# High and low halves of the moving tiles stored apart in a one-core two-block transformer kernel

## The chip, the cores and the metric

The kernel runs on one core of a Trainium2 chip. The metric is the device time of one execution in microseconds. TensorE (PE) multiplies a stationary tile of weights, loaded by its own instruction, with a moving tile that streams from SBUF, and adds into PSUM. VectorE (DVE), ScalarE (ACT) and GpSimd (POOL) work beside it, and SyncE (SP) issues the stream of weights.

## The reference

The reference is two transformer blocks over 256 tokens of width 2048 in float32. Only shapes matter for this change:

```
x:(256,2048)
block 1: h = x + fox_mixer(rms_norm(x))        16 heads of 128, causal softmax with forget decay
         h = h + conv_ffn(rms_norm(h))          up 2048 -> 2*5632, 3-tap conv, silu(gate)*val, down 5632 -> 2048
block 2: x = h + concat(gla, dilated)(rms_norm(h)) @ w_out
         x = x + (silu(h2 @ w_gate) * (h2 @ w_up)) @ w_down
```

Nearly all the arithmetic is in the products with the weight matrices.

## The kernel before

**Products.** Activations are kept transposed: 128 features on the partitions, 256 tokens (`S`) along the row. A product is needed more exactly than one pass of the fp32r format gives, so every weight tile `w` and every activation tile `x` is split into a high part and a low part, and three products are added: `w_hi*x_hi`, `w_hi*x_lo` and `w_lo*x_hi`. Line 391 does the first two in one matmul of 512 columns (256 of the high row, then 256 of the low row) into the two halves of a PSUM bank. Line 394 does the third with 256 columns, the high row alone. Such a pair is called a block here. Blocks go in groups of mostly six: six times line 391, then six times line 394 (`stretch`). The very first half unit does the same on lines 606 and 607, one block at a time.

**Weights.** They come in 784 units of 128 x 1024 through a ring of four buffers: SP loads `raw`, ACT copies it to fp32r `whi` (line 714, `split_hi`), DVE subtracts to get `wlo` (line 1038, `split_lo`), both three units ahead of TensorE. A buffer comes free when TensorE has used it (`unit_used`).

**Moving tiles.** There are three, all with a high and a low row of 256 float32 for each 128-feature chunk: `xs` (16 chunks, the normed input of a projection), `mix` (16 chunks, the heads' outputs, ahead of the output projection) and `hid2` (44 chunks, the hidden layer). ACT writes the high rows (lines 842, 931, 925, 976, 719, 760, 803, 830), DVE the low rows (lines 1061, 1136, 1197, 1269). In the profile's rows `hid2` is called hid, since numbers are left out of names.

**Addresses.** A row of one chunk is 2048 bytes in each partition: the high row, 1024 bytes, then the low row, 1024 bytes. The tile `skipped` puts the start of `xs` at 192 modulo 256 bytes (byte 82112 of each partition), and `arena` gives `hid2` and `mix` the same phase. So every high and every low row starts at 64 modulo 128 bytes, and line 391 reads 2048 bytes without a break. The tiles `whi` and `wlo` start at 128 modulo 256 bytes, and a 128-column slice is 512 bytes, so weights start at a multiple of 128.

**Order.** Each engine's program is written out by hand, in loops; semaphores tie them. There are no pools and no scheduler.

Of the kernel before, what the change touches and what calls it, by code (L numbers as in the profile page):

```python
# [27 lines left out]
F32R = mybir.dt.float32r  # L28
# [6 lines left out]
P = 128  # L35
S = 256
D = 2048
KC = D // P
FF = 5632
FC = FF // P  # L40
# [59 lines left out]
def build(nc, wstream, narrow_w, xt, vectors, identity, dist_onehot, rel_bias, gate_w2, scan_keep, gla_mask, fox_mask, out):  # L100
    with ExitStack() as ctx:
        def sb(name, shape, dt=F32):
            return ctx.enter_context(nc.sbuf_tensor(name, shape, dt))
# [6 lines left out]
        whi = [sb(f"whi{i}", [P, UW], F32R) for i in range(RING)]  # L110
# [1 line left out]
        xres = sb("xres", [P, KC, S])  # L112
        sb("skipped", [P, (X_AT - nc.sbuf_base) % PHASE // 4])
        xs_at = nc.sbuf_base
        xs = sb("xs", [P, KC, 2, S], F32R)
        folded_t = sb("folded_t", [P, S])
        vec = sb("vec", [P, VECTORS])
        ident = sb("ident", [P, P])
# [21 lines left out]
        def place(start):  # L140
            at = [start]

            def put(name, shape, dt=F32):
                t = nc.alloc_sbuf_tensor_at(name, shape, dt, offset=at[0])
                at[0] += int(np.prod(shape[1:])) * 4
                assert at[0] <= nc.sbuf_usable_end, (name, at[0])
                return t
            return put, at

        put, _ = place(arena)  # L150
        hid2 = put("hid2", [P, FC, 2, S], F32R)
        put, at_att = place(arena)
        mix = put("mix", [P, KC, 2, S], F32R)
        at_tables = at_att[0]
        decay_row = put("decay_row", [P, FOX_HEADS, S])
        qk = put("qk", [P, 2, S])
# [15 lines left out]
        put, _ = place(at_gla)  # L172
# [7 lines left out]
        put, at_sq = place(at_tables)  # L180
        sq_all = put("sq_all", [P, KC, S])
        assert at_sq[0] <= at_tables + FOX_HEADS * S * 4
        put, at_tab = place(at_tables)
# [4 lines left out]
        put, _ = place(at_gla)  # L188
# [16 lines left out]
        put, at_z = place(at_tables + FOX_HEADS * S * 4)  # L205
# [11 lines left out]
        def bank(name):  # L217
            return ctx.enter_context(nc.psum_tensor(name, [P, 512], F32))

        acc = [bank(f"acc{i}") for i in range(4)]  # L220
# [150 lines left out]
        def _(pe):  # L371
# [6 lines left out]
            def stretch(pos, blocks, x, *sizes):  # L378

                at = 0  # L380
                assert sum(sizes) == len(blocks)
                for size in sizes:
                    for k, j, bank_no, kc, opens, closes, free, late in blocks[at:at + size]:
                        if j == 0:
                            pe.wait_ge(lo_ready, pos.unit(k) + 1)
                        if free is not None:
                            pe.wait_ge(chunk_out, free)
                        if late:
                            pe.wait_ge(*late)
                        w_hi = whi[pos.slot(k)][:, j * P:(j + 1) * P]  # L390
                        pe.matmul(acc[bank_no][:, :], w_hi, x[:, kc, :, :].rearrange("p a s -> p (a s)"), start=opens, stop=False)  # L391
                    for k, j, bank_no, kc, opens, closes, free, late in blocks[at:at + size]:
                        w_lo = wlo[pos.slot(k)][:, j * P:(j + 1) * P]
                        mm = pe.matmul(acc[bank_no][:, S:2 * S], w_lo, x[:, kc, 0, :], start=False, stop=closes)  # L394
                        if j == BLOCKS - 1:
                            mm.then_inc(unit_used, 1)
                    at += size

            def half(pos, k, bank_no, part, x, late=None):
                stretch(pos, unit_blocks(k, bank_no, part, None, late), x, BLOCKS)  # L400
# [56 lines left out]
            def head(run, pos, h, k0, lag):  # L457

                n = run.count0 + h
                chunk = run.chunk0 + 3 * h  # L460
                stretch(pos, unit_blocks(k0, 1, 0, chunk - 2) + unit_blocks(k0 + 1, 1, 1), xs, 4, 6, 6)
                if lag >= 2:
                    head_values(n - 2, n)
                if lag >= 1:
                    head_scores(n - 1)
                stretch(pos, unit_blocks(k0 + 2, 2, 0, chunk - 1) + unit_blocks(k0 + 3, 2, 1) + unit_blocks(k0 + 4, 3, 0, chunk), xs,
                        4, 6, 6, 6, 2)
                if lag >= 1:
                    head_turn(n - 1)
                stretch(pos, unit_blocks(k0 + 5, 3, 1), xs, 6, 2)  # L470
                if lag >= 2:
                    pe.wait_ge(head_copied, n - 1)
                head_mean(n)
# [125 lines left out]
            def first_half():  # L599
                pe.wait_ge(first_lo, 1)  # L600
                for kc in range(BLOCKS):
                    if kc == BLOCKS // 2:
                        pe.wait_ge(lo_ready, 1)
                    pe.wait_ge(xs_ready, kc + 1)
                    cols = slice(kc * P, (kc + 1) * P)
                    pe.matmul(acc[1][:, :], whi[0][:, cols], xs[:, kc, :, :].rearrange("p a s -> p (a s)"), start=kc == 0, stop=False)
                    mm = pe.matmul(acc[1][:, S:2 * S], wlo[0][:, cols], xs[:, kc, 0, :], start=False, stop=False)
                mm.then_inc(unit_used, 1)

            first = Pos(L0.unit_heads)  # L610
            first_half()
            half(first, 1, 1, 1, xs, {8 + m: (xs_ready, 8 + m + 1) for m in range(BLOCKS)})
            narrow(0)
# [40 lines left out]
            for c in range(6):  # L654
                pe.wait_ge(chunk_out, L1.chunk_in if c == 1 or c == 2 else L1.chunk_heads + c - 2)
                for part in range(2):
                    k = 2 * c + part
# [20 lines left out]
            for j in range(2):  # L678
                chunk = DIL.chunk0 + 3 * j
                n = DIL.count0 + j  # L680
                for c in range(3):
                    pe.wait_ge(chunk_out, chunk + c - 2)
                    for part in range(2):
                        k = 2 * c + part
# [951 lines left out]
```

## Time and profile before

| | |
|---|---|
| median of 3 runs | 2258.39 us |
| the runs | 2257.77, 2258.39, 2271.72 us |
| the profiled execution | 2258.64 us |
| its span, first to last instruction | 2256.9 us |
| PE busy | 2242.0 us, 99% |
| weight loads (PEld) busy | 1968.6 us, 87% |
| DVE busy | 1617.8 us, 72% |
| ACT busy | 1226.5 us, 54% |
| POOL busy | 52.0 us, 2% |
| HBM traffic | 187 GB/s over the span |

The busy time of a matmul in the profile includes the time in which its results drain while the next one already streams, so the durations of matmuls (near 392 ns for 512 columns) overlap. What a matmul costs in a row of matmuls is the distance from its start to the next start.

### The profile page before, as it was taken

How to read it: one execution, taken by the hardware profiler on the slowest of the kernel's cores; microseconds unless marked ns; L12 is line 12 of the kernel's file. 1: busy time of each engine (PE TensorE's matmuls, PEld its weight loads, DVE VectorE, ACT ScalarE, POOL GpSimd, SP SyncE). 2: the span in 40 equal slices, each digit the busy share in tenths (PEclk: the TensorE clock that was granted, in tenths of full speed). 3: DMA queues.
4: the chain of work that ended last, by engine and by line, in shares of the span. 5: the costliest groups of instructions: out<-in, count | busy, mean ns of one | idle time of the engine just before them, and what ended most of it. 6: DMA issues, size and time to landing. Idle time of an engine off the chain costs nothing.

```text
span 2256.9 us, 38996 instructions
## 1 busy us (share of the span) xinstructions
PE 2242.0 (99%) x13138; PEld 1968.6 (87%) x13138; DVE 1617.8 (72%) x2394; ACT 1226.5 (54%) x1614; POOL 52.0 (2%) x78
## 2 busy tenths in 40 slices
PE   7999999999999999999999999999999999999999
PEld 6888888888888888888888888888888888888888
DVE  7877777788888888555567687777666666764554
ACT  6777765655555555444465577655444444443333
POOL 1111100000000000000000000000000000000000
PEclk9999999999999999999999999999999999999999
DMA  5555555555555555555545554455555555556564
GB/s 206 193 174 183 184 176 186 187 195 187 193 196 189 192 186 187 205 192 190 195 162 186 169 174 167 171 186 193 191 192 189 193 195 191 190 191 201 205 198 137
DMA packets 118598, 421.92 MB, mean 187 GB/s; under 512 B 13773, under 2 KB 15973, under 8 KB 118544
## 3 DMA queue, kind: packets, MB, share of 16 engines
q1 hardware_dynamic: 113760, 413.19, 53.8%
q0 software_dynamic: 2048, 5.42, 1.0%
q10 hardware_dynamic: 2736, 2.58, 0.4%
q8 instruction: 35, 0.57, 0.1%
q14 instruction: 19, 0.16, 0.0%
HBM read 419.01 MB, written 3.70 MB: 187 GB/s over the span
## 4 chain that ended last, share of the span: by engine, by line
PE 98%; DVE 1%; ACT 0%; DMA 0%; issue 0%; SPq 0%; DVEq 0%
PE acc L391 63%; PE acc L394 31%; PE b_score L442 0%; PE b_turn L447 0%; DMA xres<-xt 0%; PE b_mean L453 0%; PE b_mean L432 0%; PE b_mean L433 0%; PE b_val L439 0%; PE b_mean L455 0%; PE b_mean L454 0%; PE b_score L441 0%; ACT xs L842 0%; DVE wlo L1038 0%; DVE sq_all L1303 0%
## 5 line engine op out<-in xcount | busy, mean ns | idle before, releaser
L714 ACT ACTIVATE whi<-raw 128x1024 fp32r<-128x1024 f32 x783 | 825.8, 1058 | 821.4 <-PE acc L394 815.4
L1038 DVE TENSOR_TENSOR wlo<-raw,whi 128x1024 fp32r<-128x1024 f32 x783 | 959.5, 1229 | 389.3 <-ACT whi L714 386.6
L391 PE MATMUL acc<-xs,whi 128*128 128x512 f32 x4344 | 1130.7, 394 | 2.2 <-DVE wlo L1038 1.8
L391 PEld LDWEIGHTS acc<-xs,whi 128*128 128x128 f32 x4344 | 765.0, 188 | 124.7 <-DVE wlo L1038 2.9
L394 PEld LDWEIGHTS acc<-xs,wlo 128*128 128x128 f32 x4344 | 608.3, 188 | 64.8
L394 PE MATMUL acc<-xs,wlo 128*128 128x256 f32 x4344 | 620.3, 277 | 0.0
L391 PE MATMUL acc<-hid,whi 128*128 128x512 f32 x1408 | 359.9, 391 | 0.0
L1044 DVE TENSOR_REDUCE folded_t<-acc 128x256 f32<-128x512 f32 x336 | 231.4, 689 | 121.8 <-PE acc L394 110.2
L391 PEld LDWEIGHTS acc<-hid,whi 128*128 128x128 f32 x1408 | 247.2, 188 | 37.9
L394 PEld LDWEIGHTS acc<-hid,wlo 128*128 128x128 f32 x1408 | 194.2, 188 | 19.9
L394 PE MATMUL acc<-hid,wlo 128*128 128x256 f32 x1408 | 197.5, 276 | 0.0
L391 PE MATMUL acc<-mix,whi 128*128 128x512 f32 x512 | 131.5, 393 | 0.0
L391 PEld LDWEIGHTS acc<-mix,whi 128*128 128x128 f32 x512 | 90.4, 188 | 14.9 <-DVE mix L1136 0.5
L394 PEld LDWEIGHTS acc<-mix,wlo 128*128 128x128 f32 x512 | 70.6, 188 | 6.9
L394 PE MATMUL acc<-mix,wlo 128*128 128x256 f32 x512 | 71.9, 277 | 0.0
L830 ACT ACTIVATE hid<-hid 128x256 f32 (+1 forms) x88 | 36.2, 411 | 45.1 <-DVE hid L1265 44.9
L1104 DVE SCALAR_TENSOR_TENSOR qk_n<-qk,qk_gain,rstd_qk 128x256 f32<-128x256 f32 x48 | 21.6, 492 | 44.6 <-ACT rstd_qk L741 44.6
L1078 DVE TENSOR_TENSOR up_g<-folded_t,rstd 128x256 f32<-128x256 f32 x88 | 37.5, 426 | 3.0
L1078 DVE TENSOR_TENSOR up_v<-folded_t,rstd 128x256 f32<-128x256 f32 x88 | 37.5, 426 | 3.0
L1269 DVE TENSOR_TENSOR hid<-hid,hid 128x256 f32 (+1 forms) x88 | 36.9, 419 | 1.0 <-ACT hid L830 1.0
L815 ACT ACTIVATE tap_g<-up_g,vec 128x256 f32<-128x256 f32 x44 | 26.5, 603 | 16.2 <-DVE up_g L1078 16.1
L823 ACT ACTIVATE tap_v<-up_v,vec 128x256 f32<-128x256 f32 x44 | 26.5, 603 | 15.2 <-DVE up_v L1078 15.1
(195 smaller groups left out, 998.8 us busy)
## 6 DMA issues: line engine op xcount, KB each, us to landing
raw<-wstream SPq DMA_DIRECT2D x783, 512.0 KB, 3.3
decay_row<-decay_scratch POOLq DMA_DIRECT2D x16, 128.0 KB, 3.5
out<-xres ACTq DMA_DIRECT2D x16, 128.0 KB, 2.9
xres<-xt SPq DMA_DIRECT2D x3, 512.0 KB, 8.7
dist_scratch<-bias_scratch POOLq DMA_DIRECT2D x8, 192.0 KB, 4.7
toeplitz<-dist_scratch POOLq DMA_DIRECT2D x8, 128.0 KB, 3.3
xres<-xt SPq DMA_DIRECT2D x2, 256.0 KB, 4.6
raw<-wstream SPq DMA_DIRECT2D x2, 256.0 KB, 5.7
```

The costliest lines, as they stand in the source:

```text
L391: pe.matmul(acc[bank_no][:, :], w_hi, x[:, kc, :, :].rearrange("p a s -> p (a s)"), start=opens, stop=False)
L394: mm = pe.matmul(acc[bank_no][:, S:2 * S], w_lo, x[:, kc, 0, :], start=False, stop=closes)
L714: act.activation(whi[slot][:, :], raw[slot][:, :], ACT.Copy).then_inc(hi_ready, 1)
L815: act.activation(tap_g[:, :], up_g[:, 0:S], ACT.Identity, scale=column("conv0", j), bias=column("convb", j)).then_inc(tap0, 1)
L823: act.activation(tap_v[:, :], up_v[:, 0:S], ACT.Identity, scale=column("conv0", FC + j), bias=column("convb", FC + j)).then_inc(tap0, 1)
L830: act.activation(hid2[:, j, 0, :], hid[:, :], ACT.Copy).then_inc(hid_hi_ready, 1)
L1038: dve.tensor_tensor(wlo[slot][:, :], raw[slot][:, :], whi[slot][:, :], ALU.subtract).then_inc(lo_ready, 1)
L1044: dve.tensor_reduce(folded_t[0:rows, :], acc[bank_no][0:rows, :].rearrange("p (a s) -> p s a", a=2), AX_X, ALU.add).then_inc(chunk_folded, 1)
L1078: dve.tensor_tensor(dst, folded_t[0:rows, :], rstd[0:rows, :], ALU.mult).then_inc(chunk_out, 1)
L1104: dve.scalar_tensor_tensor(out=qk_n[:, a, :], in0=qk[:, a, :], scalar=qk_gain[:, col + a:col + a + 1], in1=rstd_qk[:, a, :], op0=ALU.mult, ...
L1269: dve.tensor_tensor(hid2[:, j, 1, :], hid[:, :], hid2[:, j, 0, :], ALU.subtract).then_inc(hid_split, 1)
```

## The change

Each of the three moving tiles is stored as two blocks: first all the high rows, one after another, then a gap of 64 bytes (16 elements), then all the low rows. `xs` and `mix` become 2 x (16 * 256 + 16) elements, `hid2` 2 x (44 * 256 + 16). The indexing `[:, chunk, half, :]` stays as it was, through a rearranged view. The high rows still start at 64 modulo 128 bytes, and the low rows now start at a multiple of 128 bytes. The matmuls of line 391 (and 606) read two runs of 1024 bytes, 16448 bytes apart (45120 in `hid2`), in place of one of 2048; their output is described as two halves of the same PSUM bank, at the same addresses. Line 394 reads the same kind of row as before.

Everything behind `xs` in SBUF moves by 128 bytes; `hid2` and `mix` move by 256 and keep their phase; the tiles behind `mix` move by 384. The weights' buffers and the residual `xres` stay where they are.

```
-        xs = sb("xs", [P, KC, 2, S], F32R)
+        xs = sb("xs", [P, 2, KC * S + 16], F32R)[:, :, 0:KC * S].rearrange("p a (k s) -> p k a s", k=KC)
...
-        hid2 = put("hid2", [P, FC, 2, S], F32R)
+        hid2 = put("hid2", [P, 2, FC * S + 16], F32R)[:, :, 0:FC * S].rearrange("p a (k s) -> p k a s", k=FC)
...
-        mix = put("mix", [P, KC, 2, S], F32R)
+        mix = put("mix", [P, 2, KC * S + 16], F32R)[:, :, 0:KC * S].rearrange("p a (k s) -> p k a s", k=KC)
...
-                        pe.matmul(acc[bank_no][:, :], w_hi, x[:, kc, :, :].rearrange("p a s -> p (a s)"), start=opens, stop=False)
+                        pe.matmul(acc[bank_no][:, :].rearrange("p (a s) -> p a s", a=2), w_hi, x[:, kc, :, :], start=opens, stop=False)
...
-                    pe.matmul(acc[1][:, :], whi[0][:, cols], xs[:, kc, :, :].rearrange("p a s -> p (a s)"), start=kc == 0, stop=False)
+                    pe.matmul(acc[1][:, :].rearrange("p (a s) -> p a s", a=2), whi[0][:, cols], xs[:, kc, :, :], start=kc == 0, stop=False)
```

TensorE's program has the same rows in the same order as before. On DVE and ACT only address arithmetic ahead of writes into the moving tiles differs. On DVE, in the loop of the first output projection, where the low rows of `xs` are written (line 1061), the rows with a minus are those of before:

```order
 L1038 TENSOR_TENSOR wlo<-raw,whi 128x1024
 L1060 REGISTER_ALU
-L1061 ISA x2
+L1061 ISA
+L1061 REGISTER_ALU
 L1061 SCALAR_TENSOR_TENSOR xs<-xres,vec,xs 128x256
 L1071 TENSOR_TENSOR sq_sum<-sq_sum,sq_x 128x256
```

One register instruction is of another kind; the write itself stands where it stood. The other place is DVE's write of a linear-attention head's two low rows (line 1197), which lie side by side in the new layout:

```order
 L1038 TENSOR_TENSOR wlo<-raw,whi 128x1024
 L1197 ISA x2
-L1197 TENSOR_TENSOR mix<-g_of,mix 128x2x256
+L1197 TENSOR_TENSOR mix<-g_of,mix 128x512
 L1044 TENSOR_REDUCE folded_t<-acc 128x256
 L1046 REGISTER_ALU
```

The operation has the same elements and the same place, and its pattern is one run of 512 instead of two of 256.

## Rows read from the trace of the kernel before

**Rows 1.** The page, part 1: busy time, share of the span, instructions.

```profile
PE 2242.0 (99%) x13138; PEld 1968.6 (87%) x13138; DVE 1617.8 (72%) x2394; ACT 1226.5 (54%) x1614; POOL 52.0 (2%) x78
```

**Rows 2.** The page, part 4: chain that ended last, by engine and line.

```profile
PE 98%; DVE 1%; ACT 0%; DMA 0%; issue 0%; SPq 0%; DVEq 0%
PE acc L391 63%; PE acc L394 31%; PE b_score L442 0%; PE b_turn L447 0%; DMA xres<-xt 0%; PE b_mean L453 0%; PE b_mean L432 0%; PE b_mean L433 0%; PE b_val L439 0%; PE b_mean L455 0%; PE b_mean L454 0%; PE b_score L441 0%; ACT xs L842 0%; DVE wlo L1038 0%; DVE sq_all L1303 0%
```

**Rows 3.** Waits of PE: engine, line, waited for: us in total, times, longest.

```profile
PE acc L606 <- DVE wlo L1287: 7.4, 1, 7.4
PE acc L391 <- DVE wlo L1038: 1.8, 1, 1.8
```

**Rows 4.** Waits of all engines, the longest of ACT and DVE for others.

```profile
ACT whi L714 <- PE acc L394: 815.4, 627, 3.0
DVE wlo L1038 <- ACT whi L714: 386.6, 317, 2.4
```

**Rows 5.** Groups by line: shapes xcount | busy us, mean ns | idle before, releaser.

```profile
L391 PE MATMUL acc<-xs,whi 128*128 128x512 f32 x4344 | 1130.7, 394 | 2.2 <-DVE wlo L1038 1.8 <-DVE xs L1061 0.4
...
L391 PE MATMUL acc<-hid,whi 128*128 128x512 f32 x1408 | 359.9, 391 | 0.0
...
L391 PE MATMUL acc<-mix,whi 128*128 128x512 f32 x512 | 131.5, 393 | 0.0
```

**Rows 6.** Timeline of PE in the first up projection: start us, us, what, xcount.

```profile
599.93 1.54 PE L391 MATMUL acc<-xs,whi 128*128 128x512 f32 x6
601.30 0.84 PE L394 MATMUL acc<-xs,wlo 128*128 128x256 f32 x6
601.98 1.54 PE L391 MATMUL acc<-xs,whi 128*128 128x512 f32 x6
...
610.20 1.53 PE L391 MATMUL acc<-xs,whi 128*128 128x512 f32 x6
```

**Rows 7.** Timeline of PE in the first down projection.

```profile
899.72 1.54 PE L391 MATMUL acc<-hid,whi 128*128 128x512 f32 x6
901.09 0.84 PE L394 MATMUL acc<-hid,wlo 128*128 128x256 f32 x6
901.77 1.54 PE L391 MATMUL acc<-hid,whi 128*128 128x512 f32 x6
...
903.82 1.53 PE L391 MATMUL acc<-hid,whi 128*128 128x512 f32 x6
```

**Rows 8.** Stretches: length, PE, PEld, DVE, ACT, POOL busy, granted PE clock, DMA share, GB/s.

```profile
27.00:30.00 3.00, 3.00 (x12) 2.65 (x11) 2.60 (x3) 0.00 (x0) 0.00 (x0) 0.50 0.80 233
...
606.00:612.00 6.00, 6.00 (x37) 5.26 (x36) 3.99 (x6) 2.73 (x4) 0.00 (x0) 1.00 0.57 197
```

**Rows 9.** Timeline of PE near 28 us.

```profile
28.34 1.90 PE L394 MATMUL acc<-xs,wlo 128*128 128x256 f32 x8
30.05 2.04 PE L391 MATMUL acc<-xs,whi 128*128 128x512 f32 x8
```

**Rows 10.** Timeline of weight loads in the first up projection.

```profile
605.98 1.21 PEld L391 LDWEIGHTS acc<-xs,whi 128*128 128x128 f32 x6
607.24 0.87 PEld L394 LDWEIGHTS acc<-xs,wlo 128*128 128x128 f32 x6
```

**Rows 11.** Writers of tile xs: ns min/median/max, first and last start.

```profile
L1061 DVE SCALAR_TENSOR_TENSOR xs<-xres,vec,xs x64: 476/480/489, 4.9 to 1533.2; 128x256 fp32r<-128x256 f32 x40, - x24
L931 ACT ACTIVATE xs<-xres,vec x18: 509/511/514, 363.3 to 1530.0; - x18
```

## What the change does to the time

> **What bounds the kernel now.** I read the page first. PE is busy for 99% of the span and the weight loads beside it for 87% [rows 1], and the chain of work that ended last is PE for 98%, line 391 with 63% and line 394 with 31% [rows 2]. The waits say the same from the other side: after the first 7.4 us PE waits for others hardly at all [rows 3], while ACT spends 815.4 us waiting for PE to free a weight buffer, and DVE 386.6 us waiting for ACT [rows 4]. So the time is the number of matmuls times the distance from one start to the next, and nothing else. The reader should look at that distance, since the duration in the groups by line [rows 5] includes draining.
>
> There are 4344 + 1408 + 512 = 6264 matmuls of line 391 [rows 5] and as many of line 394, besides eight pairs at the very start. In the up projection six of line 391 start at 599.93 and the six of line 394 behind them at 601.30, the next six of line 391 at 601.98 [rows 6]: 1.37 us / 6 = 228.3 ns for 512 columns, 0.68 / 6 = 113.3 ns for 256. A group lasts, over five groups, (610.20 - 599.93) / 5 = 2.054 us, or 342.3 ns for a block. In the down projection it is (903.82 - 899.72) / 2 / 6 = 341.7 ns with `hid2` as the moving tile [rows 7]. 6264 x 342.3 ns = 2144 us of the 2256.9; the rest is attention, the start and the waits.
>
> What would these matmuls take if columns alone counted? From 27 to 30 us the granted clock is 0.50, that is 1.2 GHz [rows 8], and there eight matmuls of line 394 take 30.05 - 28.34 = 1.71 us, 213.8 ns each [rows 9]. At the other level, 2.4 GHz, which is granted from 606 to 612 us [rows 8], half of it would be 106.9 ns for 256 columns and 213.8 for 512. Line 394 is at 113.3, so 6.4 ns above; line 391 is at 228.3, so 14.5 ns above. This excess is there at the high clock and, by construction of the comparison, not seen at the low one. I read it as the price of feeding four bytes a column at full rate. It is all that a new layout can give back or make worse.
>
> **The change part by part.**
>
> *What does not move.* PE's program is the same in number and order. The register instruction that ACT and DVE have more or less ahead of some writes, and the merged write of line 1197, are hidden: ACT has 815 us and DVE 387 us of waiting for weights' buffers [rows 4], and the writes into `xs` are 480 to 511 ns each, 64 of them [rows 11]. If that cover were gone, a doubled write of each of 64 low rows of `xs` would be 64 x 0.48 = 31 us on DVE, but it is spread over four projections in which DVE waits anyway. I cost this at 0. PSUM addresses are the same: 0.
>
> *Line 394.* It reads a high row from 64 modulo 128 bytes, as before. From one matmul to the next it now steps 1024 bytes and not 2048. Nothing in the trace separates the two; the 113.3 ns are the same for `xs` and for `hid2` (901.77 - 901.09 = 0.68 us [rows 7]). I take 0.
>
> *Line 391, the seam.* The 512 columns are now two runs of 1024 bytes. The trace of before has no matmul with a moving pattern of two runs. The nearest rows are those of line 394, where every 256 columns start a new run, with a new instruction too: 2 x 113.3 = 226.7 ns against 228.3. That bounds the seam from below, at -1.6 ns, or 6264 x -1.6 = -10 us. From above I bound it with as much again as a run of 256 has over its columns divided by its two ends, 6.4 / 2 = 3.2 ns: +20 us. Between them I take 0, nearer to the row of line 394, where a start that costs anything would have to be inside the 113.3.
>
> *Line 391, the low half's phase.* The low rows go from 64 modulo 128 to 0 modulo 128. Every moving row of fp32r in the trace is at 64, so the trace shows no other phase. Bounds: the low half can lose no more than its share of the excess, 14.5 / 2 = 7.3 ns, or 46 us; as much in the other direction gives +46 us. I take 0, since the excess per column is already near equal in the two lines (14.5 / 512 = 0.028 and 6.4 / 256 = 0.025 ns), which looks like a limit of the rate and not like one of the row's start.
>
> A rule of the Trainium skill bears on this, SBUF - State Buffer, Specifications: SBUF is organised in lines of 16 bytes, and speed depends on two or more accesses falling in one line. All starts, before and after, are multiples of 16, and by that rule the sum is 0 as well. It would leave no room for a phase of 64 or 128 bytes to matter at all; no run here shows that yet.
>
> *Sum:* 0 + 0 + 0, so 2256.9 us of span, and the profiled execution's 2258.64 stands 0.25 above the median of the runs, 2258.39. Forecast 2258.
>
> **The rivals.**
>
> *Faster: the low half sheds excess.* A row that starts at a multiple of 128 touches eight pieces of 128 bytes and one from 64 touches nine. If the excess of line 391 comes from the pieces, the low half loses some of its 7.3 ns. For it: the excess of line 391 is more than twice that of line 394 (14.5 against 12.8), so something in the long run of 2048 bytes costs beyond the rate. Against: eight pieces in place of nine is one ninth, not all. Half of the low half's excess gives 6264 x -3.6 = -23 us: 2235. All of it gives 2212.
> The skill's page TensorE: Matmul & The Clock Gate, Back-to-back issue gap, has N / 2.4 + 2.5 ns for an isolated matmul at the high clock, 215.8 ns for 512 columns. By it, an unhindered line 391 would save 12.5 ns of its 228.3, 78 us; the trace before does not agree, since no row of line 391 comes near it.
>
> *Slower: the low rows meet the weights.* Weights start at multiples of 128 bytes, and a weight load runs beside every matmul (six of them span 1.21 us from 605.98, and those of line 394 start at 607.24 [rows 10], each shown 188 ns long, so it reaches from the high half into the low half of a 512-column matmul). Until now moving rows and weights were never in the same phase modulo 128; now the low rows are. If two reads in the same phase delay each other, the low half's excess grows. For it: weight loads are busy 87% of the time [rows 1], so there is nearly always one to meet. Against: the two streams run at different rates, so they pass through each other's phases anyway. With half as much again as the low half's excess, +3.6 ns: +23 us, 2281; with all of it again, +46 us, 2304. It decides from 3.6 ns a matmul, which is 1%. The same holds for the seam, if two runs cost 3.2 ns: 2278.
> Against this rival stands a rule of the page TensorE: Matmul & The Clock Gate, What happens when you issue a matmul: PE has two independent read ports, and loading the next weights takes nothing from the running matmul. By it this rival's term is 0.
>
> *The change does nothing it says.* The addresses do change, so this is only the likeliest case under another name.
>
> **How the numbers follow.** About 1% (23 us) is what a measurement of this kernel can tell from no change. The likeliest, no effect beyond a few nanoseconds a block: 0.50; its own range is 2246 to 2270 (the seam from -10 us to half its upper bound). Faster rival: 0.23, of which 0.22 beyond 1%. Slower rival, phase or seam: 0.27, of which 0.26 beyond 1%, since a seam and a conflict are two ways to lose and there is one way to gain. Within 1% is 0.50 and the 0.01 that each rival leaves there, 0.52. The range must reach into both: 2222 to 2300 leaves out about 1 in 10 on either side.
>
> **What would show it.** In the up projection of the changed kernel six matmuls of line 391 should again span 1.37 us and six of line 394 0.68. With the faster rival line 391's six fall to 1.35 or less; with the slower they rise to 1.39 or more, with line 394 still at 0.68. If line 394 moves although its rows keep their phase, my reading is wrong in kind: then the step between rows or the weights' position counts. ACT's wait for PE should stay at 815 us and change only with the span. New waits of PE for DVE or ACT would mean that the writes were not covered.

## The result, and the profile after

| | before | after |
|---|---|---|
| median | 2258.18 us (2257.77 to 2271.72, 4 runs) | 2307.57 us (2307.24 to 2307.93, 4 runs) |
| span of the profiled execution | 2256.9 us | 2305.7 us |
| ratio | | 1.0183, 95% interval 1.0133 to 1.0232 |

The change makes the kernel slower, by 49 us between the medians. The forecast was 2258 with a range up to 2300, so the time lies outside it. The four times of the kernel before are three near 2258 and one at 2271.72, those of the changed kernel lie within 0.7 us.

The page of the changed kernel and its waits; the first three lines answer to [rows 1, 2], the last to [rows 4]:

```profile
PE 2291.6 (99%) x13138; PEld 1990.1 (86%) x13138; DVE 1622.8 (70%) x2394; ACT 1226.3 (53%) x1614; POOL 52.9 (2%) x78
...
PE 98%; DVE 1%; ACT 0%; DMA 0%; issue 0%; SPq 0%; DVEq 0%
PE acc L391 63%; PE acc L394 32%; PE b_score L442 0%; PE b_turn L447 0%; DMA xres<-xt 0%; PE b_mean L432 0%; PE b_mean L453 0%; PE b_mean L433 0%; PE b_val L439 0%; PE b_mean L454 0%; PE b_mean L455 0%; PE b_score L441 0%; ACT xs L842 0%; DVE wlo L1038 0%; DVE sq_all L1303 0%
```

```profile
ACT whi L714 <- PE acc L394: 867.4, 631, 3.0
```

PE's busy time has grown by 49.6 us, as much as the time. That of the weight loads has grown by 21.5 us, at the same 188 ns for one load, and of DVE by 5.0. ACT does the same work and waits 52 us longer for PE. PE waits for nobody anew. The timeline of PE in the first up projection (start us, us, what, xcount), which answers to [rows 6]:

```profile
601.44 1.56 PE L391 MATMUL acc<-xs,whi 128*128 128x512 f32 x6
602.84 0.87 PE L394 MATMUL acc<-xs,wlo 128*128 128x256 f32 x6
603.54 1.56 PE L391 MATMUL acc<-xs,whi 128*128 128x512 f32 x6
...
609.86 1.56 PE L391 MATMUL acc<-xs,whi 128*128 128x512 f32 x6
```

Six of line 391 take 1.40 us, 233.3 ns each, and six of line 394 take 0.70 to 0.71 us, 117.8 each (113.3 before). For line 391 before, the times in hundredths of a us gave the prediction 228.3 ns; the starts of the single matmuls, in nanoseconds, give 228.9 throughout the first up projection, and 233.3 now. So line 391 has lost 4.4 ns and line 394 4.5. A group takes (609.86 - 601.44) / 4 = 2.105 us, 350.8 ns for a block against 342.3. It is the same with `hid2` as the moving tile:

```profile
920.94 0.87 PE L394 MATMUL acc<-hid,wlo 128*128 128x256 f32 x6
921.65 1.56 PE L391 MATMUL acc<-hid,whi 128*128 128x512 f32 x6
923.05 0.87 PE L394 MATMUL acc<-hid,wlo 128*128 128x256 f32 x6
```

Adding the distance from start to start of all matmuls in the two traces, line 391 goes from 1447.7 to 1474.1 us and line 394 from 719.2 to 741.8. That is 26.4 + 22.6 = 49.0 us, all of the 48.8 by which the span grew. Nearly half of the loss is in line 394, whose rows start in the same phase as before. This is what had to be explained.

### The profile page after: what moved, and what is told of

It reads as the page before. It is cut to its first block, busy times and chain, and to the rows that moved or that the text cites. A ratio compares the mean times of both kernels' runs of the same rounds, so it can differ in the third digit from the quotient of the medians.

```text
span 2305.7 us, 38978 instructions
## 1 busy us (share of the span) xinstructions
PE 2291.6 (99%) x13138; PEld 1990.1 (86%) x13138; DVE 1622.8 (70%) x2394; ACT 1226.3 (53%) x1614; POOL 52.9 (2%) x78
## 3 DMA queue, kind: packets, MB, share of 16 engines
q0 software_dynamic: 2048, 5.42, 0.9%
## 4 chain that ended last, share of the span: by engine, by line
PE 98%; DVE 1%; ACT 0%; DMA 0%; issue 0%; SPq 0%; DVEq 0%
PE acc L391 63%; PE acc L394 32%; PE b_score L442 0%; PE b_turn L447 0%; DMA xres<-xt 0%; PE b_mean L432 0%; PE b_mean L453 0%; PE b_mean L433 0%; PE b_val L439 0%; PE b_mean L454 0%; PE b_mean L455 0%; PE b_score L441 0%; ACT xs L842 0%; DVE wlo L1038 0%; DVE sq_all L1303 0%
## 5 line engine op out<-in xcount | busy, mean ns | idle before, releaser
L391 PE MATMUL acc<-xs,whi 128*128 128x512 f32 x4344 | 1148.9, 399 | 2.2 <-DVE wlo L1038 1.8
L394 PEld LDWEIGHTS acc<-xs,wlo 128*128 128x128 f32 x4344 | 617.5, 188 | 69.5
L394 PE MATMUL acc<-xs,wlo 128*128 128x256 f32 x4344 | 634.5, 279 | 0.0
L391 PE MATMUL acc<-hid,whi 128*128 128x512 f32 x1408 | 366.3, 396 | 0.0
L1044 DVE TENSOR_REDUCE folded_t<-acc 128x256 f32<-128x512 f32 x336 | 231.7, 690 | 138.5 <-PE acc L394 120.5
L394 PE MATMUL acc<-hid,wlo 128*128 128x256 f32 x1408 | 203.3, 279 | 0.0
```

Source lines behind the costliest of these rows:

```text
L391: pe.matmul(acc[bank_no][:, :].rearrange("p (a s) -> p a s", a=2), w_hi, x[:, kc, :, :], start=opens, stop=False)
L1044: dve.tensor_reduce(folded_t[0:rows, :], acc[bank_no][0:rows, :].rearrange("p (a s) -> p s a", a=2), AX_X, ALU.add).then_inc(chunk_folded, 1)
```

## The experiments

"Difference" below is the start of a moving row minus the start of the weights, modulo 256 bytes. A matmul has one "run" if its 512 columns are read without a break, and two if they are two rows of 256. In the kernel before the difference is 192 - 128 = 64 for every matmul of both lines. In the changed kernel it is 64 for the high rows and 128 for the low rows.

**The gap or the separation?** The changed kernel without its 64 bytes:

```
-        xs = sb("xs", [P, 2, KC * S + 16], F32R)[:, :, 0:KC * S].rearrange("p a (k s) -> p k a s", k=KC)
+        xs = sb("xs", [P, 2, KC * S], F32R)[:, :, 0:KC * S].rearrange("p a (k s) -> p k a s", k=KC)
```

and the same for `hid2` and `mix`.

> The changed kernel without the gap of 64 bytes: high and low rows are stored apart, and all rows start at 64 modulo 128 bytes, as before. Theory 'phase of the low rows': the 49 us go with the gap, 2258 us, line 394 back at 113.3 ns from start to start and line 391 at 228 to 229. Theory 'stored apart' (the step from one row to the next, or the two runs of a matmul): the time stays near 2307, with line 394 near 118 ns.

Measured: ratio 1.0032 (0.9997 to 1.0067). The ten executions are five at 2257.6 to 2260.2, three at 2270 to 2272 and two at 2283.4, as scattered as those of the kernel before (this comes back below) and all far below 2307. The profiled one has a span of 2258.4 us, and the timeline of before is back (1.37 and 0.68 us):

```profile
601.49 1.54 PE L391 MATMUL acc<-xs,whi 128*128 128x512 f32 x6
602.86 0.84 PE L394 MATMUL acc<-xs,wlo 128*128 128x256 f32 x6
603.54 1.53 PE L391 MATMUL acc<-xs,whi 128*128 128x512 f32 x6
```

So two runs in a matmul cost nothing, and neither do high rows that lie side by side. The gap does all of it, in line 394 too: without it line 394 is at 113.3 ns although it steps 1024 bytes.

**The step between the rows of line 394.** In the kernel before:

```
-mm = pe.matmul(acc[bank_no][:, S:2 * S], w_lo, x[:, kc, 0, :], start=False, stop=closes)
+mm = pe.matmul(acc[bank_no][:, S:2 * S], w_lo, x[:, kc // 2, kc % 2, :], start=False, stop=closes)
```

> The kernel before, in which line 394 reads row k of 1024 bytes (high 0, low 0, high 1, low 1, ...) in place of the high row k, so the numbers are not the reference's; line 391 and all addresses stay. Successive matmuls of line 394 now step 1024 bytes as in the changed kernel, and not 2048. Theory 'step of the rows': line 394 rises from 113.3 to about 118 ns, +4.5 ns x 6264 = +28 us, 2286. Theory 'phase of the low rows' or anything in line 391: no change, 2258.

Measured: ratio 1.0027 (0.9998 to 1.0055), span 2254.6 us, line 394 at 0.68 us for six. Two of the eight executions are near 2256 and six at 2270 to 2272, where 7 of the 19 of the kernel before beside them lie too; none is at 2286. The step is out, a second time.

**A table of phases.** This kernel has only this loop, for each of 40 groups of 48 matmuls with a weight load each (the text on record says 34):

```
for i in range(COUNT):
    m, w = start(i), weight(i)
...
    m, w = m // 4, w // 4
...
        mm = pe.matmul(bank[:, 0:run], wt[:, w:w + P], mv[:, m:m + run], start=opens, stop=closes)
...
```

The matmuls with two runs read two rows of 256 in place of `mv[:, m:m + run]`.

> A kernel of its own that only measures (it computes nothing of the reference): 34 groups of 48 fp32r matmuls, each with its weight load, at chosen starts and steps of the moving rows and of the weights, PE alone. If the distance from start to start is set by addresses, the group with the step of 2048 bytes and start at 192 gives 113.3 ns and that with a step of 1024 gives 118, and the groups of 512 columns 229 in one run and 233 in two. If the excess over the columns comes from other engines' traffic, all groups give near 107 to 109 ns for 256 columns and 213 to 216 for 512.

> The same groups, with the weight stream of the kernel beside them (DMA of 512 KB, ACT copy, DVE subtraction for each 24 x 256 columns), into other buffers. If addresses alone count, the same numbers as with PE alone; if ACT, DVE or DMA traffic is behind the excess, 113.3, 118, 229 and 233 ns come only here.

The timeline of PE alone; the bank's letter tells one group from the next. A group's distance is the next group's start minus its own, divided by 48:

```profile
38.00 5.82 PE L109 MATMUL acc_c<-mv,wt 128*128 128x256 f32 x48
43.66 5.85 PE L109 MATMUL acc_d<-mv,wt 128*128 128x256 f32 x48
...
89.24 5.63 PE L109 MATMUL acc_e<-mv,wt 128*128 128x256 f32 x48
94.70 5.90 PE L109 MATMUL acc_f<-mv,wt 128*128 128x256 f32 x48
...
162.51 11.15 PE L109 MATMUL acc_d<-mv,wt 128*128 128x512 f32 x48
173.49 11.32 PE L109 MATMUL acc_e<-mv,wt 128*128 128x512 f32 x48
...
195.84 11.08 PE L109 MATMUL acc_g<-mv,wt 128*128 128x512 f32 x48
206.76 11.37 PE L109 MATMUL acc_a<-mv,wt 128*128 128x512 f32 x48
217.97 11.36 PE L112 MATMUL acc_b<-mv,wt 128*128 128x512 f32 x48
229.17 11.15 PE L112 MATMUL acc_c<-mv,wt 128*128 128x512 f32 x48
240.15 11.29 PE L112 MATMUL acc_d<-mv,wt 128*128 128x512 f32 x48
```

The group from 162.51 is line 391 of before (difference 64, one run): 228.8 ns. The one from 217.97 is line 391 of the changed kernel: 233.3. The one from 229.17 has two runs without the gap: 228.8. The one from 195.84 has a difference of 0: 227.5. With the weight stream beside them (DVE busy for 17.4 and ACT for 14.85 of 40 us, 185 GB/s), the same four groups start at 161.80, 217.27, 228.47 and 195.14, and take the same times within 0.3 ns. So the excess over the columns is not traffic of other engines. It is settled by where moving rows and weights start. From the distances within these groups, with the first eight of each left out, 512 columns in one run:

| difference | weights at 128, moving row shifted | moving row at 192, weights shifted |
|---|---|---|
| 0 | 226.9 ns | 226.7 ns |
| 64 | 228.9 | 228.9 |
| 128 | 232.2 | 232.6 |
| 192 | 233.4 | 233.4 |

At these four, only the difference counts, whichever side is shifted. With two runs, the first at a difference of 64, a gap of 0 gives 228.9, 64 gives 233.4, 128 gives 231.7 and 192 gives 233.3. So the low row's own difference is not the price: with a gap of 192 the low rows are at a difference of 0, the fastest in the table, and the pair costs 233.3; with the gap of 64 the mean of the table's rows for 64 and 128 would be 230.6 (an estimate), and 233.4 is measured. Both pairs cost more than either of their differences does alone.

The expectation missed one thing. The group from 38.00 should have been the only one at 118 ns, and it is (117.9). But the pattern of line 394 of before, expected at 113.3, took 117.8 here. A group with another start and a difference of 192 (from 89.24: a step of 1024, 113.3 to 113.8 ns) was at 113.3, and the same start with a step of 2048 took 117.8 in one of these two kernels and 113.3 in the other. So 256 columns have two rates at the same addresses, and what came before a group is the first suspect.

**Groups as in the kernel.** The same, with n matmuls of 512 columns and then n of 256, eight times for each of 40 patterns (38 in the text on record):

> A kernel of its own that only measures: 38 patterns of eight groups, each group like those of the kernel (n matmuls of 512 columns as on line 391, then n of 256 as on line 394), PE alone. Theory 'the state is handed on': in the pattern of before line 394's matmuls take 113.3 ns, in that of the changed kernel 118, although the rows that they read start in the same phase; the same pattern gives the same numbers wherever it stands. With weights of line 391 in the phase of the moving rows (difference 0 modulo 256) 227 ns and not 229. Theory 'chance of the entry': the pattern of before gives 113.3 in one place of the sequence and 118 in another. With the low rows 192 bytes further in place of 64, 233 and 118 again.

Timeline of the pattern of before (bank b), of the changed kernel (c), and of before once more (d):

```profile
49.19 1.53 PE L107 MATMUL acc_b<-mv,wt 128*128 128x512 f32 x6
50.56 0.84 PE L113 MATMUL acc_b<-mv,wt 128*128 128x256 f32 x6
51.24 1.54 PE L107 MATMUL acc_b<-mv,wt 128*128 128x512 f32 x6
...
63.67 1.56 PE L110 MATMUL acc_c<-mv,wt 128*128 128x512 f32 x6
65.07 0.87 PE L113 MATMUL acc_c<-mv,wt 128*128 128x256 f32 x6
65.77 1.56 PE L110 MATMUL acc_c<-mv,wt 128*128 128x512 f32 x6
...
78.39 1.53 PE L107 MATMUL acc_d<-mv,wt 128*128 128x512 f32 x6
79.76 0.87 PE L113 MATMUL acc_d<-mv,wt 128*128 128x256 f32 x6
80.47 1.53 PE L107 MATMUL acc_d<-mv,wt 128*128 128x512 f32 x6
```

Bank b shows the kernel's 1.37 and 0.68 us. Bank c shows 1.40 and 0.70. Bank d has the instructions of bank b, but line 394's six take 0.71 us: it keeps the 118 ns that it found, through all eight groups. Both theories had half of it: what comes before decides, and it persists. With the other gaps (0, 128, 192) line 394 is at 117.8 on the mean as well, but these were all entered at 118, and the one without a gap is at 113 in the kernel of the first experiment, so they show nothing on line 394.

**Weights of line 391 at a difference of 0.** In the kernel before, `whi` is moved to 192 modulo 256 and `wlo` stays at 128:

```
+        sb("skipped_hi", [P, (HI_AT - nc.sbuf_base) % PHASE // 4])
         whi = [sb(f"whi{i}", [P, UW], F32R) for i in range(RING)]
+        sb("skipped_lo", [P, (LO_AT - nc.sbuf_base) % PHASE // 4])
         wlo = [sb(f"wlo{i}", [P, UW], F32R) for i in range(RING)]
```

> The kernel before, with the buffers of the high weights moved to 192 modulo 256 bytes, so that in line 391 moving rows and weights differ by 0 modulo 256, while line 394 keeps its difference of 64. Theory 'phase of moving against weights': line 391 from 229 to 227 ns, -2 ns x 6264 = -13 us, 2245, if line 394 stays at 113.3; if the state in which line 391 leaves the engine decides line 394's rate, 394 may go to 118 and the kernel to 2271.

Measured: 2278.44 us, ratio 1.0052 (1.0028 to 1.0077; beside it the kernel before had most of its times near 2270), twelve times within 0.8 us. Neither number was met. Line 394 went to the slow rate, as the second one had it (739.2 us in sum, 719.2 before), but line 391 gained 0.7 ns in the projections and nothing in sum (1447.5 us), where the 2 ns of groups of 48 in a row had been expected. The timeline in the up projection:

```profile
601.38 0.87 PE L398 MATMUL acc<-xs,wlo 128*128 128x256 f32 x6
602.08 1.53 PE L395 MATMUL acc<-xs,whi 128*128 128x512 f32 x6
603.45 0.87 PE L398 MATMUL acc<-xs,wlo 128*128 128x256 f32 x6
```

Six of line 394 (here 398) take 0.70 us. The same pattern, in groups of six, had been in the measuring kernel beside it: 228.2 + 117.3 ns for a block against 228.9 + 113.3, +3.3 ns x 6264 = +21 us on the fastest executions of before (2256 to 2258), 2278. This sum was made afterwards. The group size belongs to the pattern: in groups of eight the same addresses took 233.8 + 117.9 ns in the measuring kernel, in groups of twelve 227.4 + 117.6.

**Everything moved together** (moving tiles at 0, all weights at 192, modulo 256):

> The kernel before with everything of the product moved together: moving tiles at 0 modulo 256 bytes in place of 192, both weights at 192 in place of 128, so their difference stays at 64. Theory 'only the difference between moving rows and weights counts': 2258, 229 and 113.3 ns. Theory 'a row's own start counts' (0 modulo 128 as the low rows of the changed kernel): slower by 49 us or more.

Measured: ratio 0.9966 (0.9936 to 0.9996), no slowdown although all rows of this kernel start at a multiple of 128. Its ten executions lie at 2256.4 to 2258.4 (seven) and 2270.5 to 2272.0 (three), and the profiled one is of the second kind, 2270.47. Its timeline at two places:

```profile
1001.93 0.84 PE L396 MATMUL acc<-hid,wlo 128*128 128x256 f32 x6
1002.61 1.54 PE L393 MATMUL acc<-hid,whi 128*128 128x512 f32 x6
1003.98 0.84 PE L396 MATMUL acc<-hid,wlo 128*128 128x256 f32 x6
...
1801.95 0.87 PE L396 MATMUL acc<-xs,wlo 128*128 128x256 f32 x6
1802.65 1.55 PE L393 MATMUL acc<-xs,whi 128*128 128x512 f32 x6
1804.04 0.87 PE L396 MATMUL acc<-xs,wlo 128*128 128x256 f32 x6
```

In the first layer line 394 (here 396) has its 0.68 us. In the second it has 0.70 to 0.71, and line 391 (here 393) 1.39 in place of 1.37. From 1439 us to the end every group of line 394 is slow but for six groups of eight; line 391 is back at 228.9 ns from 2150 us on. Against the profiled execution of the kernel before, line 391 sums to 1449.5 us (1447.7) and line 394 to 729.5 (719.2), which is 12.1 us where the span is 11.8 longer. This most likely explains the scatter of the kernel before too. Its 77 executions beside the timed experiments are 42 at 2256 to 2260 us, 31 at 2269 to 2274 and 4 at 2284 to 2285: the 118 ns pattern in neither, one or (so I read it) both layers. Of those at 2270 and 2284 there is no profile of the kernel before itself.

**What ends a pattern?**

> A kernel of its own that only measures. First part: the pattern of before with groups of n = 3 to 16, each entered behind the pattern of the changed kernel and four groups of six in which line 394's matmuls take 118 ns. Theory 'two states, and the length of a group decides whether one is left': with n = 3, 6, 9, 12 (multiples of the period of three in which the distances repeat) a slow state stays, 118; with other n it goes over to 113.3 and stays there, also in the six groups of six behind. Theory 'only the entry counts': 118 with every n. Second part: line 391 alone, moving rows at 0 to 224 modulo 256 and weights at 128, low rows 16384 plus 0, 64, 128 or 192 bytes behind the high ones: 227 ns at a difference of 0 without a gap, 229 at 64, 233 for every gap of 64 modulo 128 at a high row that differs by 64.

Groups of 3, 9 and 12 kept the 118 ns that they were entered with, as expected. Other sizes did not settle at 113 ns; they went back and forth. With n = 8 the groups alternated 113, 118, 113, 118. The second part has line 391 alone. Without a gap it takes 226.9 ns at a difference of 0 and 228.9 at 64, as before, but 232 to 234 at 32, 96, 128, 160, 192 and 224. With a gap no pair of differences came below 229.9 ns, and most were at 233 (all with the first eight left out). So it is not enough that both rows have the same difference: of the eight tried, only 0 and 64 are fast.

**Groups of eight in the kernel before and in the changed kernel** (all sizes of six in the three projections replaced):

```
-                    stretch(Pos(layer.unit_up + 8, 24, i), units(3 * i + 1, 0, 24), xs, *[6] * 32)
+                    stretch(Pos(layer.unit_up + 8, 24, i), units(3 * i + 1, 0, 24), xs, *[8] * 24)
```

> The kernel before with groups of eight in place of six in the output, up and down projections, which take most of the time. Theory 'two states': no execution stays in the slow state, so the times bunch near 2257, where the kernel before has some near 2257 and some near 2271 us. If groups of six were better for another reason: all slower, and bunched.

> The changed kernel with groups of eight in place of six in the output, up and down projections. Theory 'the low rows at another phase leave only the slow state': line 394 stays at 118 ns with any size of group and the time at 2307 us (within 3). Theory 'the changed kernel merely entered the slow state and groups of six kept it': line 394 falls to about 116 on the mean, as it does in the kernel before with groups of eight, and the time to about 2294.

The first, in the up projection:

```profile
699.98 1.07 PE L394 MATMUL acc<-xs,wlo 128*128 128x256 f32 x8
700.88 1.99 PE L391 MATMUL acc<-xs,whi 128*128 128x512 f32 x8
702.71 1.11 PE L394 MATMUL acc<-xs,wlo 128*128 128x256 f32 x8
703.66 2.00 PE L391 MATMUL acc<-xs,whi 128*128 128x512 f32 x8
```

Eight of line 394 take 0.90 us, the next eight 0.95, and so on: 113 and 118 in turns, as the measuring kernel has it. All eleven executions lie between 2266.38 and 2268.86, so bunched as expected, but midway and not at 2257 (ratio 1.0023, 0.9999 to 1.0047). The changed kernel in groups of eight gave 2307.97 and 2307.98, ratio 1.0223 (1.0193 to 1.0253), and in the measuring kernel its pattern kept no 113 ns in groups of 1, 2, 4, 6, 8 or 12. That excludes that it merely entered a bad pattern which its groups of six then kept.

Yet its line 394 can run at 113 ns. In the trace of the changed kernel one group of it does, behind a distance of 295 ns in line 391:

```profile
1483.45 1.07 PE L394 MATMUL acc<-mix,wlo 128*128 128x256 f32 x8
1484.36 2.03 PE L391 MATMUL acc<-mix,whi 128*128 128x512 f32 x8
1486.22 1.10 PE L394 MATMUL acc<-mix,wlo 128*128 128x256 f32 x8
```

Eight take 0.91 us, and the next eight, behind an undisturbed run of line 391, 0.95 again. So the addresses of line 394 don't forbid the fast rate; the runs of line 391 with the gap, whose distances go 229, 238, 229, 238 and not 226, 229, 232, don't lead to it.

**The rule of handing on.** 330 groups of random size, 110 in each of three layouts:

> A kernel of its own that only measures: three series of 110 groups of random size (2 to 12), PE alone. Series 1 is the layout of before, series 2 has the weights of line 391 in the phase of the moving rows, series 3 also those of line 394 at a difference of 192. Theory 'a state is handed from group to group': within a series the distance in line 394's matmuls is 113.3 or 118 by whole groups, a group of 6, 9 or 12 keeps what was before it, and the other sizes change it by a fixed rule; then a sequence of sizes can be found that ends in the fast state from every state. If it were chance, the same size behind the same state would give both.

Each group has n matmuls of line 391 and then n of line 394. In the layout of before, every one of the 110 groups follows one rule. The distances in line 391 have a period of three: 226, 229, 232 ns. If a run of line 391 ends behind its 232, line 394 takes 113.3 ns (0.90 us for eight at 41.84 below), otherwise 118 (0.95 at 32.15). Behind a 113 ns run line 391 starts again with 226.

```profile
32.15 1.10 PE L106 MATMUL acc_b<-mv,wt 128*128 128x256 f32 x8
33.10 2.23 PE L100 MATMUL acc_c<-mv,wt 128*128 128x512 f32 x9
...
41.84 1.07 PE L106 MATMUL acc_e<-mv,wt 128*128 128x256 f32 x8
42.74 2.45 PE L100 MATMUL acc_f<-mv,wt 128*128 128x512 f32 x10
```

In the table, "118, to 233" means that line 394 takes 118 ns and that the next run of line 391 starts with a distance of 233; "stays" means that it starts as this one did.

| line 391 starts with | group of 3k | of 3k + 1 | of 3k + 2 |
|---|---|---|---|
| 226 (behind 113 ns) | 113, stays | 118, to 233 | 118, to 229 |
| 229 | 118, stays | 118, to 235 | 113, to 226 |
| 233, 236 | 118, stays | 113, to 226 | 118, to 235 |
| 235, 231 (or 232) | 113, to 226 | 118, to 233 | 118, to 229 |

Groups of six keep whatever they are entered with in the first three rows, the good and the bad. Under this rule no sequence of equal pairs leads to the 113 ns pattern from every start. Unequal ones do: with runs of line 391 in multiples of three, the 113 ns pattern survives any number of matmuls of line 394 behind it, and from both slow patterns (229 and 233) a number of 3k + 1 leads on to the fast one within three groups. This last was worked out from the table, by how far each run gets in the period of three; no group there had unequal numbers. In the other two layouts (line 391 at a difference of 0) 15 and 11 of the 110 groups had 113 ns, against 44, and a block took 347.2 and 347.4 ns against 345.4.

**A kernel from the rule.** The kernel before, with `size, size_lo` in `stretch` and

```
+PULL = [(6, 4), (6, 7), (6, 7)]
-                    stretch(Pos(layer.unit_up + 8, 24, i), units(3 * i + 1, 0, 24), xs, *[6] * 32)
+                    stretch(Pos(layer.unit_up + 8, 24, i), units(3 * i + 1, 0, 24), xs, *PULL * 10, 6, 6)
```

and likewise in the other up groups, the down projections and the output projections' loop. It is the same work, in a slightly different order.

> The kernel before with the same matmuls, in which most groups of six and six in the output, up and down projections are replaced by six of line 391 and 4, 7 and 7 of line 394. By the rule that the series of random sizes gives (the fast state survives groups of line 391 that are multiples of three, whatever follows; from a slow state a number of line 394's matmuls that is 1 modulo 3 leads on to the fast state within three groups), the slow state can't last. Theory 'handed-on state': all executions near 2256 to 2258 us, where the kernel before has some at 2270 to 2284. If the rule holds only in a program of PE alone: times as scattered as before, or one value above 2258.

```profile
601.31 0.96 PE L396 MATMUL acc<-xs,wlo 128*128 128x256 f32 x7
602.10 1.54 PE L393 MATMUL acc<-xs,whi 128*128 128x512 f32 x6
603.48 0.62 PE L396 MATMUL acc<-xs,wlo 128*128 128x256 f32 x4
603.93 1.53 PE L393 MATMUL acc<-xs,whi 128*128 128x512 f32 x6
```

Seven take 0.79 us, four 0.45, 113 ns each. All twelve executions lie between 2256.08 and 2259.80, while those of the kernel before beside them were 9 at 2256 to 2259, 7 at 2269 to 2272 and one at 2285.3. The ratio is 0.997 (0.9945 to 0.9995). It doesn't beat the best execution of the kernel before; it takes away the bad ones, of which a kernel that scattered like the one before (8 of 17) would have had none in twelve with a chance below 0.1% (9/17 to the twelfth power, an estimate).

## Why the prediction was wrong

*What bounds the kernel* was right: PE's start-to-start distance is the time, before and after, and all 49 us are in it. *PE's program, the writes of ACT and DVE, the register instructions* at 0: right, no new wait. *The seam* at 0: right, 228.8 ns with one run and with two.

*Line 391, the low half's phase*, was taken as 0 because the excess per column is nearly equal in the two lines. That inference failed. It measured +4.4 ns in the projections and 26.4 us in sum, inside the bound of 46 us that the text had. Equal excess at one phase says nothing on another phase.

*Line 394* was the larger error, since it had no bound at all: "it reads a high row from 64 modulo 128 bytes, as before", so 0. It measured +4.5 ns in the projections and 22.6 us in sum. It is less than 6264 x 4.5 = 28 us, since in the head loops line 394 of before is at 118 ns part of the time, as here (0.71 us for six):

```profile
154.57 0.87 PE L394 MATMUL acc<-xs,wlo 128*128 128x256 f32 x6
155.28 1.09 PE L391 MATMUL acc<-xs,whi 128*128 128x512 f32 x4
```

The step assumed that a matmul's rate depends on its own operands. The runs showed that it also depends on where line 391's pattern of three ends ahead of it, and that pattern is gone once the low rows stand at another difference than the high ones.

*The slower rival* named the place (low rows against weights) and had a price of 23 to 46 us for line 391, in which the 26.4 us fall, but held line 394 at 0.68 us. Its mechanism, that two reads in the same phase modulo 128 bytes delay each other, is not what the runs show: at a difference of 0 moving rows and weights are in the same phase too, and that is the fastest of all, 226.9 ns. That its price for line 391 fits is luck. With both terms bounded, the range would have reached 2258 + 46 + 28. The slower side beyond 1% had a chance of 0.26; the rows of before could not tell the sign, but the range was cut short for want of the second term. (A slip beside it: from -10 to half of +20 us the likeliest case would reach from 2248 to 2268, and not from 2246 to 2270.) The check "if line 394 moves although its rows keep their phase, my reading is wrong in kind" was the one that came true. Its own alternatives (the step between rows) were not it either, and the weights' position was half of it.

The faster rival's price rested on pieces of 128 bytes that a row touches. With everything moved together to start at multiples of 128 the fast executions stayed at 2256.4 to 2258.4, so nothing was gained and such pieces don't count.

Of the rules weighed: by the 16-byte lines of the Trainium skill, SBUF — State Buffer, Specifications, 64 bytes could not matter; they do, 228.9 against 233.4 ns. By the Trainium skill, TensorE: Matmul & The Clock Gate, What happens when you issue a matmul, loading the next weights takes nothing from the running matmul; moving only the weights' start changes 512 columns from 226.7 to 233.4 ns, so where the weights are read does bear on the matmuls' time. The measurements decide in both.

What stays open: what inside the engine makes the period of three and the two rates of 256 columns. The runs give the rule, not the mechanism. That moving rows meet the weight load in time would fit a rate that depends on their difference, but was not shown.

## What to carry to other kernels

When PE is busy without a gap, the sum is in the distance from start to start, so read that from the timeline and not the durations, and give every group of matmuls on the path a bound of its own, even one whose operands a change doesn't touch. Keep both halves of a matmul's moving rows at one difference from the weights modulo 256 bytes, and at one that was measured to be fast (here 0 or 64, and for the pair of lines 391 and 394 in groups of six 64). Measure phases in a small kernel that has nothing but the matmuls, but in the real kernel's order and group sizes: groups of six gave the real 2278 us, while groups of 48 in a row had promised 2245. If a kernel's times come in clumps, compare the start-to-start distance stage by stage before blaming the chip.

## What the runs showed of the hardware that I had not expected

- fp32r matmuls of 512 columns with a weight load each, 24 or 48 in a row, take 226.7 to 235.1 ns at the high clock, by how the moving rows' starts differ from the weights'. None came to the 213.8 ns that the rows at the low clock would give at the high one.
- In short groups with matmuls of 256 columns between them, what came before counts as well: at the addresses of before, groups of six take 228.8 or 230.8 ns for each matmul of 512 columns.
- Matmuls of 256 columns at a difference of 64 have two rates, 113.3 and 117.8 ns, at the same addresses. Which one holds is handed from group to group by a rule without exception in 110 groups, and the slow one lasted for over 700 us without a break in one execution.
- At a difference of 0, where 512 columns are fastest (226.9 ns), 256 columns are slow (120.0 ns, 48 in a row).
